# Joined two-block kernel: filler matmuls, first pad copies and an output projection's first unit take other places

## The reference, cut to what matters

```python
h = rms_norm(x, norm_g[i, 0]) * (1 + sc1) + sh1          # first block
y, yc = hybrid_mixer(h, hc, rows, not last, w_in[i], conv_p, ssd_p, fourier_out[i], rwkv_p, w_o[i])
x = x + g1 * rms_norm(y, norm_g[i, 1])
h = rms_norm(x, norm_g[i, 2]) * (1 + sc2) + sh2
x = x + g2 * rms_norm(sq_relu_mlp(h, mlp_up[i], mlp_down[i]), norm_g[i, 3])
...
h = rmsnorm(x, g_mix[l]) * (1.0 + sc1) + sh1             # second block
x = x + gt1 * hybrid_mixer_2(h, w_in[l], ...)            # pooling, 8 heads of attention, RG-LRU, @ w_out
h = rmsnorm(x, g_ffn[l]) * (1.0 + sc2) + sh2
x = x + gt2 * conv_glu_ffn(h, w_ffn_gate[l], w_ffn_up[l], ffn_conv_w[l], ffn_conv_b[l], w_ffn_down[l])
return rmsnorm(x, final_g)
```

## Time and profile before

| | |
|---|---|
| three runs | 3496.0, 3499.29, 3501.36 us, median 3499.29 |
| the profiled execution | 3493.42 us, its span 3491.7 us |
| granted TensorE clock, mean | 0.981 |
| busy: PE, DVE, ACT, POOL | 3309.5 (95%), 2163.0 (62%), 1185.5 (34%), 175.9 (5%) us |
| weight loads (PEld) | 2719.5 us (78%) |
| DMA | 706.31 MB, mean 202 GB/s |

### The profile page before, as it was taken

One profiled execution on the slowest core, in us unless ns is written; L12 is line 12 of the kernel. 1 busy time (PEld: TensorE's weight loads), 2 busy tenths in 40 slices (PEclk: granted clock), 3 DMA queues, 4 the chain that ended last, 5 costly groups with the idle time before them and its releaser, 6 DMA issues.

```text
span 3491.7 us, 57711 instructions
## 1 busy us (share of the span) xinstructions
PE 3309.5 (95%) x23026; PEld 2719.5 (78%) x23026; DVE 2163.0 (62%) x3268; ACT 1185.5 (34%) x1550; POOL 175.9 (5%) x280
## 2 busy tenths in 40 slices
PE   6898999989999999998999999998999899999998
PEld 3674576457777799997888888886888788888887
DVE  2174665663332466566787878788656767767767
ACT  2111121022222322234444344444444543444344
POOL 0000000101211100000000000000000000000000
PEclk9999999999999999999999999999999999999999
DMA  9844635722111387754676767673444456656654
GB/s 366 328 157 156 247 130 198 288 110 83 56 57 56 112 343 292 273 223 156 227 280 241 279 240 275 244 267 126 153 157 159 175 184 236 236 185 228 230 185 151
DMA packets 99134, 706.31 MB, mean 202 GB/s; under 512 B 10992, under 2 KB 10992, under 8 KB 17776
## 3 DMA queue, kind: packets, MB, share of 16 engines
q1 hardware_dynamic: 74736, 523.27, 41.0%
q0 software_dynamic: 23184, 169.88, 12.9%
q10 hardware_dynamic: 1008, 10.23, 0.7%
HBM read 697.05 MB, written 6.29 MB: 201 GB/s over the span
## 4 chain that ended last, share of the span: by engine, by line
PE 82%; DVE 7%; issue 4%; ACT 3%; DMA 3%; POOL 1%; DVEq 0%; ACTq 0%; POOLq 0%; SPq 0%
PE ps L2319 28%; PE ps L2318 14%; PE ps L535 10%; PE ps L954 5%; PE ps L2054 3%; PE ps L355 2%; PE ps L1534 2%; PE ps L2315 2%; PE ps L2036 2%; PE ps L2035 2%; PE ps L2037 2%; PE ps L1525 2%; ACT rows_parts L2278 1%; PE ps L2316 1%; DMA ring<-in_conv_u 1%
## 5 line engine op out<-in xcount | busy, mean ns | idle before, releaser
L2319 PE MATMUL ps<-hT_parts,rows_parts 128*128 128x512 f32 x3210 | 1130.9, 394 | 0.0
L2318 PE MATMUL ps<-hT_parts,ring_parts 128*128 128x256 f32 x3210 | 900.9, 281 | 0.3 <-DVE hT_parts L2292 0.3
L2283 DVE TENSOR_TENSOR ring_parts<-ring,rows_parts 128x2048 fp32r<-128x2048 f32 (+1 forms) x340 | 769.9, 2264 | 206.7 <-ACT rows_parts L2278 205.8
L2278 ACT ACTIVATE rows_parts<-ring 128x2048 fp32r<-128x2048 f32 (+1 forms) x340 | 643.6, 1894 | 412.5 <-DMA ring<-in_mlp_u 167.6
L2319 PEld LDWEIGHTS ps<-hT_parts,rows_parts 128*128 128x128 f32 x3210 | 603.9, 188 | 126.0
L2318 PEld LDWEIGHTS ps<-hT_parts,ring_parts 128*128 128x128 f32 x3210 | 608.7, 190 | 10.3 <-DVE hT_parts L2292 0.6
L2319 PE MATMUL ps<-work_parts,rows_parts 128*128 128x512 f32 x1616 | 573.7, 396 | 0.0
L2318 PE MATMUL ps<-work_parts,ring_parts 128*128 128x256 f32 x1616 | 453.0, 280 | 2.3 <-DVE work_parts L2506 2.3
L535 PE MATMUL ps<-hT,ring 128*128 128x512 f32 (+1 forms) x1088 | 376.0, 507 | 16.9 <-ACT work L802 12.6
L2319 PEld LDWEIGHTS ps<-work_parts,rows_parts 128*128 128x128 f32 x1616 | 303.5, 188 | 68.6
L535 PEld LDWEIGHTS ps<-hT,ring 128*128 128x128 f32 x1088 | 206.6, 191 | 184.7 <-issue 173.1
(11 more groups left out here) (442 smaller groups left out, 3818.5 us busy)
## 6 DMA issues: line engine op xcount, KB each, us to landing
ring<-in_mlp_u SPq DMA_DIRECT2D x128, 1024.0 KB, 4.9
ring<-in_ffn_u SPq DMA_DIRECT2D x88, 1024.0 KB, 4.8
rows<-in_mod_r POOLq DMA_DIRECT2D x64, 1024.0 KB, 5.5
ring<-in_gate_u SPq DMA_DIRECT2D x64, 1024.0 KB, 7.0
work<-in_ada_r POOLq DMA_DIRECT2D x64, 1024.0 KB, 5.1
ring<-in_in_u SPq DMA_DIRECT2D x36, 1024.0 KB, 4.8
ring<-in_mod_u SPq DMA_DIRECT2D x32, 1024.0 KB, 7.6
rows<-in_ada_r POOLq DMA_DIRECT2D x32, 1024.0 KB, 8.3
```

Source lines behind the costliest of these rows:

```text
L2278: act.activation(unit_high(u)[:, 0:size], slot(u)[:, 0:size], ACT.Copy).then_inc(hi_done, 1)
L2283: dve.tensor_tensor(ring_parts[:, u % SLOTS, 0:size], slot(u)[:, 0:size], unit_high(u)[:, 0:size].bitcast(F32), ALU.subtract)\
L2318: pe.matmul(ps[:, b, low_half], low, top(kt), start=False, stop=False)
L2319: mm = pe.matmul(ps[:, b, :], high, both(kt), start=False, stop=kt == kts - 1)
```

## The change

It has six parts.

- `SsdIn`: `scalar_norm` is cut in two. The copies of pair 3's banks (`first_pads`) stand between them, and the loop skips these. `pads` is cleared ahead of the centring. `cmu` and `crs` move in SBUF.
- A column stands behind every third tap of the convolution instead of every sixth; `RwIn` has fewer.
- `RwScan`: `fill(pe, 3)` between the two first-level squares, `fill(pe, 1)` in place of 2 behind levels 0 to 2 of the half squares, and 6 in place of 3 in half rounds in front of `nv`'s reader.
- `In2`: logits and values of the last head go ahead of the weighing of the one before, and the output projection's first unit is issued in three pieces around its turn and weighing; the other units follow in `Ffn2`.
- `Ffn2`: `rest_unit` stands behind `scale_split`, the memset of `gpad` goes to POOL.
- The end: DVE multiplies 14 of 16 output tiles, POOL two, and there are five output DMAs.

```diff
@@ class ConvFft
         csq = w(c2 + CT * T, CT * T, a=CT)
-        cmu = w(c2 + 2 * CT * T, T)
-        crs = w(c2 + 2 * CT * T + T, T)
+        cmu = w(C0 + 9760, T)
+        crs = w(C0 + 9760 + T, T)
...
                 act.activation(flat(csq), flat(cacc), ACT.Square).then_inc(conv_sq, 1)
+
+            def scalar_root(act, own):
                 full(act, use_var)
...
-                    if k % 6 == 2:
+                    if k % 3 == 2:
                         first_columns(dve, 1)
 
             def vector_norm(dve, own):
+                own.step(dve.memset(pads.rearrange("p r c t -> p (r c t)"), 0.0))
+                own.settle()
+                dve.sem_inc(pad_zero, 1)
...
+        def first_pads(act, o):
+
+            ins = act.activation(pads[:, o, :, 2:2 + T], ps[:, o, :].rearrange("p (c t) -> p c t", c=2), ACT.Copy)
+            emptied(ssd_uses[3][o], ins)
@@ class SsdIn
                 ConvFft.scalar_norm(act, own)
+                unit_done(act, seg_ssd + 7)
+                act.wait_ge(pad_zero, 1)
+                for o in range(2):
+                    first_pads(act, o)
+                ConvFft.scalar_root(act, own)
...
-                        if t == 0:
-                            act.wait_ge(pad_zero, 1)
                         if t >= 2:
                             act.wait_ge(conv5, t - 1)
+                        if n == 3:
+                            continue
...
-                own.step(dve.memset(pads.rearrange("p r c t -> p (r c t)"), 0.0))
-                own.settle()
-                dve.sem_inc(pad_zero, 1)
@@ class RwIn
-                    first_columns(dve, (2, 2, 3, 3, 3, 3, 1, 0)[n])
+                    first_columns(dve, 1 if n < 2 else 3 if n < 6 else 0)
@@ class RwScan
                             squares(x[h], Q, Tm)
+                            if n == 0 and h == 0:
+                                fill(pe, 3)
                         fill(pe, 2)
...
-                        fill(pe, 2)
+                        fill(pe, 1 if n < 3 else 2)
...
-                    fill(pe, 3)
+                    fill(pe, 6 if half else 3)
                     evacuated(pe, u["at"])
@@ def unit_products
-        def unit_products(pe, u, use, x, off=0, it=None, k=0, kts=KT, split=None, ready=None):
+        def unit_products(pe, u, use, x, off=0, it=None, k=0, kts=KT, split=None, ready=None, first=0, last=None):
...
-            pe.wait_ge(w_split, off + (u - SPLIT0 + 1))
-            acquire(pe, use, it, k)
-            for kt in range(kts):
+            if first == 0:
+                pe.wait_ge(w_split, off + (u - SPLIT0 + 1))
+                acquire(pe, use, it, k)
+            for kt in range(first, kts if last is None else last):
...
-            mm.then_inc(w_used, 1)
+            if last is None:
+                mm.then_inc(w_used, 1)
@@ class In2
+        def out2_first(pe, first, last):
+
+            unit_products(pe, seg_out2, (0, use_out2[0][1]), high_then_low(hT_parts), split=3 * KT, first=first, last=last)
...
+                Head.logits(pe, AH - 1)
+                Head.turn_values(pe, AH - 1)
                 Head.weigh(pe, AH - 2)
-                Head.turn_values(pe, AH - 1)
-                Head.logits(pe, AH - 1)
+                out2_first(pe, 0, 8)
                 Head.turn(pe, AH - 1)
+                out2_first(pe, 8, 12)
                 Head.weigh(pe, AH - 1)
+                out2_first(pe, 12, None)
@@ class Ffn2
+        POOL_PART = KT - 2
+        OUT_PARTS = ((0, 4), (4, 8), (8, 12), (12, POOL_PART))
...
-                for n in range(0, KT, 4):
-                    sp.wait_ge(out_done, n + 4)
-                    sp.dma_start(out_t[:, n:n + 4, :], xT[:, n:n + 4, :]).then_inc(x_in, 16)
+                for n, (first, last) in enumerate(OUT_PARTS):
+                    if n == 2:
+                        sp.wait_ge(pool_tiles, 3)
+                        sp.dma_start(out_t[:, POOL_PART:, :], xT[:, POOL_PART:, :]).then_inc(x_in, 16)
+                    sp.wait_ge(out_done, last)
+                    sp.dma_start(out_t[:, first:last, :], xT[:, first:last, :]).then_inc(x_in, 16)
...
-                to_width(pe, seg_out2, use_out2, high_then_low(hT_parts), 3 * KT)
+                for j in range(1, 4):
+                    unit_products(pe, seg_out2 + j, (j % 2, use_out2[j % 2][1] + j // 2), high_then_low(hT_parts))
+                with pe.Fori(1, KT // 4) as it:
+                    for j in range(4):
+                        unit_products(pe, seg_out2 + j, (j % 2, use_out2[j % 2][1] + j // 2), high_then_low(hT_parts), it * 4, it, 2)
...
-                pool.memset(flat(y4), 0.0).then_inc(y_zero, 1)
+                pool.memset(flat(y4), 0.0).then_inc(pool_tiles, 1)
+                pool.memset(gpad.rearrange("p r t -> p (r t)"), 0.0).then_inc(gpad_zero, 1)
                 pool.wait_ge(x_split, 4 * KT + 1)
                 fetch_late(pool, LATE_ROWS, GATE_ROWS)
+                pool.wait_ge(nrs, rms_x4.k)
+                pool.tensor_tensor(xT[:, POOL_PART:, :], xT[:, POOL_PART:, :], bc(rtn, KT - POOL_PART), ALU.mult).then_inc(pool_tiles, 1)
...
-                own.step(dve.memset(gpad.rearrange("p r t -> p (r t)"), 0.0))
-                own.settle()
-                dve.sem_inc(gpad_zero, 1)
-                rest_unit(dve, seg_ffn[0] + AHEAD_DVE)
                 rms_x3.vector(dve)
                 scale_split(dve, 2, gffn, adaT[:, 3 * KT:4 * KT])
+                rest_unit(dve, seg_ffn[0] + AHEAD_DVE)
                 dve.sem_inc(gact, 2)
                 dve.wait_ge(nadd, 3 * KT)
-                dve.wait_ge(y_zero, 2)
+                dve.wait_ge(pool_tiles, 2)
+                dve.wait_ge(gpad_zero, 1)
...
-                for kt in range(0, KT, 4):
-                    part = xT[:, kt:kt + 4, :]
-                    dve.tensor_tensor(part, part, bc(rtn, 4), ALU.mult).then_inc(out_done, 4)
+                for first, last in OUT_PARTS:
+                    part = xT[:, first:last, :]
+                    dve.tensor_tensor(part, part, bc(rtn, last - first), ALU.mult).then_inc(out_done, last - first)
```

8 lines of the change are left out of this document (4 added, 4 removed).

## The result

The changed kernel took 3471.7 us as the median of four runs (3471.06 to 3474.66); the kernel before, in four, 3497.64 (3494.94 to 3501.36). The ratio is 0.9929, with a 95% interval of 0.9914 to 0.9945: 25.9 us faster, where 31.1 were forecast (3468, range 3456 to 3484).

A forecast was written before the change was run, and what follows sets the result against it. PE, busy 95% of the span, was taken as the bound, so only its idle or half-clock stretches pay. Terms 11.4 + 2.4 + 9.4 + 5.5 + 1.5 + 0.9 = 31.1 off 3499.3 gave 3468 us, range 3456 to 3484.

The forecast's parts named there:

- A: Second mixer's projection (SsdIn): earlier bank copies remove PE's 9.48 us wait and 1.9 of low clock, 11.4 us.
- B: RwIn: one column fewer on DVE in a chain PE waits for, wait 7.7 to 5.3, 2.4 us.
- D: Last head and output projection's first unit: 6.6 us of PE waits saved if the clock holds, else 3.0; taken 5.5.
- E: Norm before the FFN: reciprocal no longer waits behind a weight unit's split, 1.5 us.
- C: RwScan, eight rounds: fillers moved into PE's waits for POOL and for nv's copy, 9.4 us.
- F: End: POOL takes two of 16 output tiles and the last DMA halves, 0.9 us; by the skill's rule -1.3.
- Rival 2: Covers run out: convolution columns wait for rows, clock stays low, half-round fills overrun; 3479 us; 0.26 shared with another rival.
- instruction supply: RwScan's dense 64x64 products: stops read as late instructions behind weight traffic; moved fetches could bring or cost 4 us, taken 0.
- Rival 1: Instruction supply gets better: the two stops in dense products and slow fills behind them vanish, 10 more, 3458 us; chance 0.14.
- Rival 3: Slower than before: PE's instructions come late in all eight rounds' dense products, six new stops cost 32 us; chance 0.05.

The follow-up runs named there:

- x5_hold_fetches: Changed kernel with the old end, three fills in half rounds, and SP holding weight fetches in full rounds until the dense products are done: median 3457.2 us.
- y4_hold_only: Kernel before, with only the weight fetches held back in full rounds until the dense products are done: median 3487.3 us, ratio 0.9969.
- x1: Changed kernel with the end as before: DVE multiplies all 16 output tiles in four products, POOL none, four output DMAs; median 3469.0 us.
- x2: Changed kernel with five output parts of 4, 4, 4, 2 and 2 tiles, all on DVE, none on POOL; median 3468.2 us.
- x7: Changed kernel, but DVE waits for POOL's product at the end before it begins its four; median 3468.8 us.

## Why the prediction was right

It was right in direction and size (25.9 us measured, 31.1 forecast), and of its six terms four were right (A, B, D, E), one was too high (C) and one had the wrong sign (F). One pair of profiles is not enough to size a term, so the table has beside it the difference of the means of all profiles that have the same program in the stretch, without the edit (two or three) and with it (two to eleven):

| us | A | B | C | D | E | F | sum |
|---|---|---|---|---|---|---|---|
| forecast | 11.4 | 2.4 | 9.4 | 5.5 | 1.5 | 0.9 | 31.1 |
| the two profiles | 9.1 | 2.1 | 6.7 | 5.8 | 1.8 | -1.3 | 24.2 |
| the means | 12.1 | 2.0 | 6.3 | 6.7 | 1.9 | -1.3 | 27.7 |

By the means C was 3.1 too high and F 2.2; D, 1.2 too low, and A made up for a part of it, which is luck.

- **A: 11.4 forecast.** The term is exact: from L588 (185.71) to pair 4's first L535 (283.46) it takes 97.75 us, against 107.40 before, 9.65 less, and the clock behind it holds too (1.00 where it was 0.53), since L758 comes 11.5 earlier relative to L588 (246.2 against 257.7). Behind L758, some 165 us after the copies, PE meets DVE's columns, whose rows come by DMA. There the wait is 1.5 or 3.6 us without the change and 1.0 to 4.8 with it, so the 9.1 of the first pair is chance at this place and no failure of the term. What the prediction didn't look at is that this chain was there to be had: two columns moved away from it gave 4.1 us. Rival 2 had named the mechanism, at the wrong place.
- **B: 2.4 forecast, 2.1 measured**; the wait went from 7.7 to 5.4 as stated.
- **C: 9.4 forecast, 6.7 measured.** The levels gave 1.24 in each of eight rounds, 9.9 of 10.7. Half rounds 4 and 6 lost 0.5 each, the 1.0 of the text, and Merge's start won nothing: a wait of 7.5, forecast 7.7. The mis-sized term is the one that I had set to 0, instruction supply: rounds 1, 3, 5 and 7 took -1.2, +0.7, +1.2 and +1.1 us in the dense products, 1.9 in all and 2.3 with the fills behind them. It lies inside the 4 us that I had allowed, but the reading behind it was half wrong. Round 1 gained as argued: its instruction packet came 1.1 us earlier. In round 5, "as before", the third fetch went from 0.3 to 2.9 us ahead of the dense products, 2.5 us nearer to the two ahead of it. But the stop stayed as long (3.15 and 3.13); the 1.2 are the products behind it, which ran at a clock of 1.00 before and of 0.50 now. PE runs on at 1071.99, the clock is 0.50 from 1072, and it still is over the fills (clock, DMA share and GB/s at the end):

```profile
1074.00:1077.00 3.00, 3.00 (x20) 2.47 (x17) 0.00 (x0) 2.12 (x4) 0.00 (x0) 0.50 0.00 0
```

In rounds 3 and 7 PE ran out 0.4 and 0.7 us earlier in the stretch and the packet landed 0.5 and 0.4 later; in round 7 a third fetch now stands 4.2 us ahead. The Trainium skill (Runtime: NRT & Kernel Launch, Instruction fetch mechanics) has instruction fetch hidden; x5_hold_fetches, y4_hold_only and the packets show that it is not where 2 to 3 MB of weights are fetched just ahead of a dense stretch of short matmuls.
- **D: 5.5 forecast, 5.8 measured**, and the second unit 6.8 us earlier relative to the head before (its turn), 6.7 by the means: the 6.6 of the text, which I had marked down for the clock. The better end was the true one: the clock stayed at 1.00 through the whole stretch, in which PE stood still for 0.8 us at most.
- **E: 1.5 forecast, 1.8 measured** over the FFN's stretch. The reciprocal (2709.17) follows the root (2708.66 + 0.47) at once, and PE's wait for the norm's first output (L2351, L2335 before) is 4.2 us where it was 5.7.
- **F: 0.9 forecast, -1.3 measured.** The step that failed is the reading of the earlier trace rows: POOL's products next to DVE's there took at most 0.92 us, from which I took it that the two run side by side. The weighing went against the rule cited there, and the rule gives -1.3. The trace of before shows what these neighbours were. POOL's product starts at 780.02 with 0.32 us left of a DVE product of two operands in SBUF (L1792, 779.72 to 780.34), and takes 0.91 us; the next DVE product beside it (L1790, 780.26 to 780.67) reads one of its two operands from PSUM. Where no DVE product is beside it, POOL's takes 0.72. The 0.2 may so be a wait for the rest of the first; this I argue only, no run parts the two. At the end both start together, on products with both operands in SBUF, and DVE has to wait for all but 0.14 us of the other. x1, x2 and x7 settle it: the rule of the Trainium skill (SBUF — State Buffer, Who interferes with whom) holds here, and the smaller last DMA is worth nothing.

The rest, +1.9 in Mlp and +0.9 at the start, is in no edit's reach; the medians moved by 25.9 rather than 21.3. Rival 1 did not come, but could be had: the stops shrink to 0.1 to 0.8 us when the fetches are moved on purpose, which gives 9 us. Rival 3 (long stops in all rounds) did not occur; the four half rounds, which have no dense stretch of this length, had no such stop in any profile, so its count of eight was wrong, too.

What stays open: why PE's wait for ACT at the end of stretch A swings between 1.0 and 4.8 us from one execution to the next; and why the clock falls behind some of the stops and not behind others of the same length.

## What to carry to other kernels

A gain has to be followed past the next buffer to whatever is paced by DMA, and behind such a chain one pair of profiles doesn't size it: two executions of the same program differed there by 4 us, so read the term ahead of the chain, or the means of several profiles. Where an engine stops with nothing to wait for, look at the bulk transfers issued a few microseconds ahead and at the packets of the instruction queue, and move the transfers rather than the work: here a wait of three lines was worth some 9 us, nearly as much as the largest edit. Before an elementwise product is shared out between DVE and GpSimd, one look at the two side by side tells whether they overlap at all.
